# Two transformer blocks in one kernel: every stage laid out by one rough clock

## The reference

```python
def first_block(x, ...):
    u = rmsnorm(x, norm_mix_pre)
    z = u @ w_in            # pool input 512, q, k, v 512 each, two gates of 1024
    pool = pool_mixer(p, pool_w, pool_scale)           # 4 windows
    att = moba_attention(q, k, v)                      # 8 heads of 64, alibi, causal
    mix = sigmoid(gate0) * (pool @ w_branch_pool) + sigmoid(gate1) * (att @ w_branch_attn)
    h = x + rmsnorm(mix @ w_out, norm_mix_post)
    return h + rmsnorm(relu(rmsnorm(h, norm_mlp_pre) @ w_up)**2 @ w_down, norm_mlp_post)

def second_block(h, p, ...):
    for i in range(2):
        hn = rms_norm(h, attn_norm[i])
        h = h + (diff_attention(hn) if i == 0 else windowed_gqa(hn))
        h = h + conv_ffn(rms_norm(h, ffn_norm[i]), ...)   # gated, conv of width 3
        gate = sigmoid(rms_norm(h, ple_norm[i]) @ ple_w_gate[i])
        h = h + (p[i] @ ple_w_proj[i]) * gate
    return rms_norm(h, final_norm)
```

## Time and profile before

| | |
|---|---|
| median of 3 runs | 2112.64 us (2110.96 to 2117.57) |
| profiled execution | 2110.71 us |
| its span | 2108.9 us |
| PE busy | 1991.0 us, 94% |
| DVE, POOL, ACT busy | 56%, 52%, 42% |
| granted clock of TensorE, mean | 0.98 |

### The profile page before, as it was taken

The page is one execution under the profiler, slowest core; times in us unless marked ns, Lnnn a source line. Parts: engine busy times, 40 slices in busy tenths (PEclk is TensorE's granted clock), DMA queues, the critical chain, the costliest instruction groups (busy, mean ns, idle before and its releaser), DMA issues.

```text
span 2108.9 us, 25618 instructions
## 1 busy us (share of the span) xinstructions
PE 1991.0 (94%) x9428; PEld 1626.9 (77%) x9428; DVE 1183.7 (56%) x2003; ACT 889.4 (42%) x1689; POOL 1090.3 (52%) x843
## 2 busy tenths in 40 slices
PE   6999997999999799999999999988999899999986
PEld 5787885788888677777788888876778788888875
DVE  4763215243332678776774466456676674664555
ACT  4544333433343345543544343344565444343342
POOL 4335445444445474663565565544864475656541
PEclk9999998999999899999999999999999999999998
DMA  4112231232223111111232322322101223323221
GB/s 146 55 66 90 90 100 60 88 108 97 99 83 111 67 56 47 61 60 62 89 100 90 107 94 83 117 71 86 51 31 51 88 92 100 100 80 110 94 76 50
DMA packets 48652, 174.36 MB, mean 83 GB/s; under 512 B 5392, under 2 KB 5776, under 8 KB 48528
## 3 DMA queue, kind: packets, MB, share of 16 engines
q1 hardware_dynamic: 48528, 172.73, 24.8%
HBM read 170.61 MB, written 2.10 MB: 82 GB/s over the span
## 4 chain that ended last, share of the span: by engine, by line
PE 80%; DVE 13%; issue 3%; ACT 2%; DMA 1%; POOL 0%; SPq 0%; DVEq 0%; ACTq 0%; POOLq 0%
PE b L388 24%; PE b L390 23%; PE b L389 23%; PE b L410 2%; DVE ssq L480 2%; DVE ra L474 1%; PE b L402 1%; PE b L422 1%; PE b L421 1%; PE b L423 1%; PE b L440 1%; DVE h L675 1%; PE b L431 1%; DVE h L719 1%; DVE fa L689 1%
## 5 line engine op out<-in xcount | busy, mean ns | idle before, releaser
L234 POOL TENSOR_TENSOR ra<-raw,ra 128x512 fp32r<-128x512 f32 x632 | 861.3, 1381 | 852.6 <-ACT ra L274 852.1
L388 PE MATMUL b<-ra 128*128 128x512 f32 x2528 | 1008.4, 399 | 64.8 <-DVE ra L474 36.9
L390 PE MATMUL b<-ra 128*128 128x512 f32 x2528 | 991.7, 392 | 0.0
L389 PE MATMUL b<-ra 128*128 128x512 f32 x2528 | 991.6, 392 | 0.0
L388 PEld LDWEIGHTS b<-ra 128*128 128x128 f32 x2528 | 479.4, 190 | 177.7 <-issue 43.1
L390 PEld LDWEIGHTS b<-ra 128*128 128x128 f32 x2528 | 478.9, 189 | 102.9
L389 PEld LDWEIGHTS b<-ra 128*128 128x128 f32 x2528 | 479.8, 190 | 93.9
L274 ACT ACTIVATE ra<-raw 128x512 fp32r<-128x512 f32 x632 | 382.0, 625 | 328.1 <-PE b L390 288.4
L604 DVE TENSOR_TENSOR tmp<-b,rb 128x512 f32<-128x512 f32 x81 | 55.4, 691 | 186.1 <-PE b L390 185.9
L689 DVE TENSOR_TENSOR fa<-b,fa 128x512 f32<-128x512 f32 x136 | 90.5, 687 | 80.4 <-PE b L390 79.9
L597 DVE TENSOR_TENSOR ra<-b,ra 128x512 fp32r<-128x512 f32 (+4 forms) x166 | 92.0, 569 | 50.4 <-ACT ra L327 31.4
(11 more groups left out here) (238 smaller groups left out, 1830.6 us busy)
## 6 DMA issues: line engine op xcount, KB each, us to landing
raw<-in_f_g SPq DMA_DIRECT2D x40, 512.0 KB, 3.5
raw<-in_f_v SPq DMA_DIRECT2D x40, 512.0 KB, 3.5
raw<-in_f_d SPq DMA_DIRECT2D x40, 512.0 KB, 3.5
raw<-in_w_up SPq DMA_DIRECT2D x32, 512.0 KB, 3.5
raw<-in_w_down SPq DMA_DIRECT2D x32, 512.0 KB, 3.5
raw<-in_p_g SPq DMA_DIRECT2D x16, 512.0 KB, 3.5
raw<-in_w_gp SPq DMA_DIRECT2D x8, 512.0 KB, 3.5
raw<-in_w_ga SPq DMA_DIRECT2D x8, 512.0 KB, 3.4
```

Source lines behind the costliest of these rows:

```text
L234: e.tensor_tensor(wl, src, wh.bitcast(F), ALU.subtract).then_inc(*w_low.mark(n))
L388: e.matmul(ps, wh[:, c:c + 128], xh, start=start, stop=False)
L389: e.matmul(ps, wh[:, c:c + 128], xl, start=False, stop=False)
L390: last = e.matmul(ps, wl[:, c:c + 128], xh, start=False, stop=stop)
```

## The change

The arithmetic is the same, tile by tile. `linear`'s hooks, `later`, `tick`, `flush`, `pending` and `queue_inputs` are gone. Norms, convolutions, gates, residuals and PLE results are now processes like the heads, and one `Flow` runs over the whole kernel. `columns` and `spread` are PE steps with rank -2, ahead of any head's. The combined rows are cut: `parts` into `round` and `rest`, `square_add` into the square and `sum_square`, `ple` into `scaled_out`, `sigmoid`, `times` and `residual`. A sum of squares goes to POOL or DVE, whichever clock is behind (the last always DVE). Durations of the rough clock are finer (0.85 us for DVE work in SBUF, 1.5, 3.0 or 3.7 for longer forms). The first matmul group after an attention's first projections uses bank 6. The last quarter of an attention's output product has groups of 2 tiles instead of 4. ACT loads its table in a `warm` row ahead of everything, and the hold for the alibi load is gone; the mask is waited for where it is used.

```diff
@@ scalar_program
+        if kind == "warm":
+            w.wait_ge(*a[0])
+            e.activation(m.sm[:, 94:95], m.ones[:, 0:1], ACT.Copy).then_inc(*act.mark(n))
@@ vector_program
-        elif kind == "ple":
-            j, b, z, y, rb, copied, free, h_done, mm_done = a
...
-            e.tensor_tensor(z, banks[b][:, :], m.rb[:, :], ALU.mult).then_inc(*evac.mark((n, 0)))
-            w.wait_ge(m.sig("act"), n)
-            w.wait_ge(*copied)
-            e.tensor_tensor(z, z, y, ALU.mult).then_inc(*evac.mark((n, 1)))
...
-            e.tensor_tensor(m.h[:, j, :], m.h[:, j, :], z, ALU.add).then_inc(*evac.mark(n))
+        elif kind == "times":
+            z, y, made, copied = a
+            w.wait_ge(*made)
+            w.wait_ge(*copied)
+            e.tensor_tensor(z, z, y, ALU.mult).then_inc(*els.mark(n))
@@ duration
-    return 0.69
+    if kind == "conv_two":
+        return 3.0 if a[5] is None else 3.7
...
+    return 0.69 if engine == "ac" or kind in PSUM_READS else 0.85
@@ build
-                    if hooks and step in hooks:
-                        hooks[step]()
...
-                    tick(3 * G)
+    def square(x, src, made):
+        yield 0, "ac", lambda: (made,) if x["n"] == 0 or (x["sum"] and T.free) else None
...
+        i, q, free = T.get()
+        s = done("ac", "square", row("square_of", q, src, made, free))
+        yield 0, "v", lambda: (s, x["sum"])
+        eng = "v" if x["left"] == 1 else x["sums"] or ("p" if sc.clock["gp"] + 0.5 < sc.clock["ve"] else "v")
+        n = row("sum_square", q, s, x["sum"], eng)
...
+    def root(x):
+        yield -2, "pe", lambda: None if bank_free[STB] is None else (x["sum"], *bank_free[STB])
+        v = rstd_cols(m.ssq, (x["sum"],), 1024.0, 0)
+        stat["sum_free"] = now("pe")
+        yield -2, "pe", lambda: None if bank_free[STB] is None else (v, *bank_free[STB])
+        x["spread"] = t = spread(0, v)
@@ the PLE gate's results, in ffn2
-            n = row("ple", j, b, z, y_chunk(j), stat["rb"], pl[j], f1, h_tok[j], tok)
+                i, z, v = yield from scaled(pn, b, tok, 2)
+                yield 0, "ac", lambda: (v,)
+                s = done("ac", "act", row("sigmoid", z, None, v))
+                yield 0, "v", lambda: (s, pl[j])
+                v = done("ve", "elem_v", row("times", z, y_chunk(j), s, pl[j]))
+                v = done("ve", "evac", row("residual", h[:, j, :], z, (v,), h_tok[j]))
@@ attention outputs
-    a[name + "a"], a[name + "b"], a[name + "c"] = lay(w[:512], 1), lay(w[512:768], 2), lay(w[768:], 4)
+    a[name + "a"], a[name + "b"], a[name + "c"] = lay(w[:512], 1), lay(w[512:768], 2), lay(w[768:], 2)
```

More of the change, by code:

```diff
@@ L1084, in cols_now, with norm @@
[L1084 to L1094 removed]
+    def norm(slots, sums=None):
+        return dict(slots=slots, tok=[None] * NC, n=0, sum=None, rb=None, spread=None, last=False, sums=sums)
@@ L1839, in f @@
-                tiles.append((one, two, three))
-                if len(tiles) == ntile:
-                    ts = list(tiles)
-                    tiles.clear()
-                    for s in range(ntile + 2):
-                        later(lambda s=s: [ts[s - z][z]() for z in (2, 1, 0) if 0 <= s - z < ntile])
-                return (v,)
-            return f
-        tiles = []
-        g_buf = [m.gbuf[:, q, :] for q in range(4)]
-        back = T.take_back(NT)
-        T.lend([cr, sr], *now("ve"), *now("gp"))
@@ L2000, in build @@
+    flow.run(whole())
     assert plan is None or st["used"] == total
```

1314 lines of the change are left out of this document (633 added, 681 removed).

## The result

The changed kernel takes 2094.22 us (median of 4 runs, 2090.10 to 2096.14) and the kernel before 2114.3 us in the same comparison; the ratio is 0.9903, with a 95% interval of 0.988 to 0.9925. The change is faster by some 20 us. The forecast was 2066 us in a range of 2049 to 2094, so the direction was right, and less than half of the gain came.

A forecast was written before the change was run, and what follows sets the result against it. PE bounds the kernel, with 118 us idle, mostly at joints where it waits for DVE. Terms sum to -46.7 us from 2110.7, so 2064.0 profiled and 2066 us for the median; range 2049 to 2094.

The forecast's parts named there:

- What bounds the kernel: Whole kernel: PE busy 1991.0 of 2108.9 us; the 118 us idle lie at joints between stages, `ffn2` itself is full.
- Start: First 50 us: without the alibi hold and with an early table load, first matmul near 9.3 instead of 15.72; -7.4 us.
- Post-norms: Both post-norm joints: +1.8 for earlier `columns` and later first product, -2.1 after the value-tile wait is covered; -0.3 us.
- Ends of `ffn2`: Ends of both `ffn2`: PE's 5.96 us wait for the last sum of squares goes, with the clock dip; -8 us each.
- norm of `ffn2(0)`: Window from 975, 7.1 us idle: last group of 2 tiles lets inputs begin earlier; -3 us, of 0 to -7.
- POOL's sums give the gain back: Rival at joints: sums moved to POOL lengthen DVE rows by 1.1 us each, losing 12 us: 2078; chance 0.17.
- PLE gate: PLE gate and sliding norm, from 1420: four banks read at once, so the 9.21 us bank wait goes; -11 us.
- Sliding heads: Attention stages: heads were laid by the same clock before, so 0 us, with -5 and +5 as ends.
- Norm of `ffn2(1)`: In the window from 1470, 8.2 us idle: same edits as for `ffn2(0)`; -5 us, of -1 to -8.
- end: Kernel's end, where PE waits 8.23 us for the last sum: batching shortens the chain; -4 us, of 0 to -6.
- Waits for sums of 5 us that remain: Sign in the changed profile that would make the forecast wrong; it expected no `columns` wait behind `ffn2` over 2 us.
- Only simple things work: Rival: only start and PLE batching pay (7.4 + 11), each other joint finds a new last wait: 2094; chance 0.12.

The follow-up runs named there:

- that experiment: Changed kernel with PE taking a `columns` step only when the rough clock has its sum ready for 3 us (0.2 as changed): 2068.82 us, ratio 0.9789 to before.
- the kernel with 4 us: Changed kernel with `columns` 4 us late and the low part of sliding attention's query tiles on DVE instead of POOL: 2062.25 us, ratio 0.976 to before.

## Why the prediction was wrong, point by point

**What bounds the kernel.** Right: both `ffn2` stayed full, and all of the gain and loss lies at joints and heads.

**Start, -7.4.** Measured -3.9. The step that failed is "the first matmul can begin at 10.7 ... to 9.4 or so": it stands at 11.16.

```profile
9.17 2.51 DVE L464 SCALAR_TENSOR_TENSOR ra<-h,vec,ra 128x512 fp32r<-128x512 f32 x2 [9.17 <-ACT ra L288]
...
7.98 2.50 POOL L234 TENSOR_TENSOR ra<-raw,ra 128x512 fp32r<-128x512 f32 x2 [6.51 <-ACT ra L275]
...
11.16 0.77 PE L380 MATMUL b<-ra 128*128 128x512 f32 x1 [11.16 <-DVE ra L464]
```

DVE's first low part starts at 9.17, close to the forecast's time, but takes 1.85 us, since one of POOL's first splits (7.98 to 10.48) falls on it; in the kernel without the splits it takes 0.75, and the first matmul follows 0.90 us after its start instead of 1.99. The distance of 1.1 us that I had taken came from a row on which a split fell as well, but only with its last 0.4 us (it ran from 13.76 to 15.03), and the row took 0.95:

```profile
14.62 0.95 DVE L474 SCALAR_TENSOR_TENSOR ra<-h,vec,ra 128x512 fp32r<-128x512 f32 x1 [14.62 <-DMA mask<-in_alibi]
```

The other part is luck of the profiled execution. ACT's first split starts when the first weights have landed, at 7.20 us here and at 6.18 to 6.94 in the eleven other traces of the changed kernel's variants without the hold. In two of them, the kernel with the sums on DVE and the one with the query on DVE, the rows of the start are those of the changed kernel: the first matmul stands at 10.29 and 10.91, `columns` at 48 doesn't wait (2.0 us here), and the start takes 36.6 and 37.4 us. Against 43.1 before that is -6.5 and -5.7, inside the bounds of the forecast.

ACT's table load now ends at 2.01. The Trainium skill ("ScalarE: Activation LUTs", "What ACT_TABLE_LOAD costs") adds a drain as long as the load. Neither trace shows one: the next instruction of ACT began at 7.84 behind a load that ended at 7.82 before, and begins at 2.02 now.

**Post-norms, -0.3.** Measured +1.0, each part near its term. The wait for the value tile is gone as forecast; a wait of 4.1 us at `columns` stands in both joints where there was none, and the first ends with one of 2.4 for the low part of a weight. I saw that `columns` stood earlier than its sum and priced it at 1.8 us; I didn't ask what it would be worth to place it later. The second post-norm alone falls by 5.2 us in that experiment.

**Ends of `ffn2` (-16) and norm of `ffn2(0)` (-3).** Measured -7.2 and +0.2. The step that failed is "So the wait of 5.96 goes, and with it the dip of the clock": at both ends 2.2 us of the wait remain, PE is idle 4.9 us where it was 7.7, and the granted clock of the stage is 0.96 and 0.98, after 0.93 and 0.96. The 12 matmuls of cover gave their 2.7 us; "Four of the seven sums leave DVE", counted at 2.7 to 7.1, gave at most the 1.1 us by which the wait fell further, since the chain to the last sum still runs beside the splits: without them, and with `columns` in the same place, the wait is 0. With `columns` another 12 matmuls later (the kernel with 4 us) the wait is 0, the clock 1.00 and the two ends take 43.2 and 73.1 us, that is -7.6 and -7.7 against the kernel before: what the forecast had. So what was missing is the place of `columns`, which the rough clock chose too early for a chain whose rows take 1.7 us. In the norm of `ffn2(0)` 12 matmuls later give 3.2. The rival "POOL's sums give the gain back" had one thing right: moving the sums wins nothing at the ends (47.3 and 77.0 us with all of them on DVE). It had the larger cause, the place of `columns`, no more than the forecast did. The Trainium skill ("SBUF — State Buffer", "SBUF: two separate sides") says that DVE and POOL take a shared pair of ports as a lock for a whole instruction. The 1.77 us of a sum beside POOL's splits and 0.68 without them agree with it; these runs don't show whether it is a lock or something else.

**PLE gate, -11.** Measured -5.6. The wait of 9.21 us for a bank is gone, as forecast. In its place stands a wait of 5.35 at `columns`, which I hadn't looked for, and the clock of the stage is 0.95 as before. The forecast asked what was late now, and not what is late next: the products and residuals that come behind the batch, several of them at 1.7 us. The step that failed is "The wait goes, with 1.3 of slow clock": one wait went and another came. With `columns` at 5340 instead of 5316 there is none, the clock is 1.00, and the stage takes 58.5 or 57.2 us, which is -12.4 and -13.7.

**Sliding heads, 0 with -5 to +5.** Measured +10.2, outside its bounds. The step that failed is "Their heads were laid by the same clock before; 0". With the norm and the gate in the same flow the clock lays these heads anew. PE has the same instructions in the stage, but its first P times V comes after 5511 large matmuls, where it was 5490 (5475 with the query's low part on DVE), so fewer projections are left to fill the gaps of the later heads. The order is at fault for the most part and not the splits, since 6.0 of the 10.2 us are lost without them too.

**Norm of `ffn2(1)`, end.** -3.5 for -5 and -3.9 for -4: right.

**Range.** Its lower end, "2049 (the forecast with start, ends and PLE at their better ends)", doesn't follow from the terms: these better ends are 0.6, 3.8 and 2 us below the forecast, which makes 2060.

**Signs.** "Waits for sums of 5 us that remain" was named as a sign that the forecast is wrong, and it came. The rival "Only simple things work" had the time, 2094, mostly by luck: it wanted a new last wait at each joint, for a weight's low part or an input. One joint found a weight late, by 2.4 us; the others waited for the same sums.

What stays open: which placement of the heads' rows costs the sliding stage its 8 to 10 us; that was undone by an edit, not isolated. Open too is what the sums on POOL cost with `columns` held in its place, since no kernel held it. The profiled execution of the kernel with the sums on DVE is only 10.6 us below the changed one's where the medians are 16 apart, so its account by stage is incomplete.

## What to carry to other kernels

When a scheduler with a rough clock lays in-order queues, a row that reduces or synchronises, placed too early on the engine that bounds the kernel, costs its whole wait; placed 12 or 24 matmuls later it cost nothing in most of these joints, and 9 us in the differential heads. Give such rows a margin of their own, and choose it by joint. Take the durations for the clock from contended rows, since 0.85 instead of 0.69 did nothing and 1.25 gave 19 us. Bringing more stages under the same scheduler also moves the stages that it already laid, so put bounds of their own on them.

## What the runs showed of the hardware

The subtraction of the low parts, 512 columns at 1.3 to 1.8 us each and 632 of them, hides nearly everywhere from PE (in the changed kernel PE waits for one of them, 2.4 us), yet without it the two kernels are 58 and 64 us of 2100 faster. That it acts through DVE's rows beside it shows in the sum of 1.77 and 0.68 us; POOL's own later rows, which then stand behind fewer splits, have a share in it that these runs don't tell. The start of a kernel has the same contention within its first ten microseconds (1.85 us for the first low part, 0.75 without the splits).

Rows of DVE that read a bank don't suffer from it. In the changed kernel the same addition takes 0.69 us on average with an input from a bank and 1.01 to 1.13 with both in SBUF; in the kernel without the splits it is 0.69 and 0.82 to 0.87. The groups of the changed kernel (mean ns behind the busy time):

```profile
L700 DVE TENSOR_TENSOR h<-b,h 128x512 f32<-128x512 f32 x48 | 32.5, 688 | 15.3 <-PE b L382 15.1
L700 DVE TENSOR_TENSOR h<-gbuf,h 128x512 f32<-128x512 f32 x7 | 7.9, 1132 | 0.2
```
